# Deferring the second layer norm to the outputs of the first two feed-forward units

## The reference, cut to what matters

```python
h = memory_cross_attention(x, mem, xa_wq, xa_wkv, xa_wo)       # ends with "@ wo"
x = layer_norm(ALPHA * x + h, ln2_g, ln2_b)                    # the second norm
u = causal_dwconv(x @ w_up, conv_w, conv_b)                    # 3 taps, 5632 columns
g, val = split(u); h = (gelu(g) * val) @ w_down
x = layer_norm(ALPHA * x + h, ln3_g, ln3_b)                    # the third norm
```

## Time and profile before

| | us |
|---|---|
| median of 3 runs | 903.06 |
| lowest, highest | 900.4, 904.37 |
| the profiled execution | 901.49 |
| its span, first to last instruction | 899.7 |

### The profile page before, as it was taken

One profiled execution on the slowest core, in us unless ns is written; L12 is line 12 of the kernel. 1 busy time (PEld: TensorE's weight loads), 2 busy tenths in 40 slices (PEclk: granted clock), 3 DMA queues, 4 the chain that ended last, 5 costly groups with the idle time before them and its releaser, 6 DMA issues.

```text
span 899.7 us, 15840 instructions
## 1 busy us (share of the span) xinstructions
PE 857.0 (95%) x6396; PEld 807.8 (90%) x6396; DVE 651.3 (72%) x1011; ACT 503.2 (56%) x723; POOL 7.6 (1%) x17
## 2 busy tenths in 40 slices
PE   8989998999899999999997989999899899999997
PEld 7869987889799999999996989898899899999886
DVE  5765697678668888887867896687797866665453
ACT  5644447355447666655446657777657654444442
POOL 0200000000000000000000000000000000000000
PEclk9989999989998999999988999999999799999999
DMA  9973567747062766567752576475575276775751
GB/s 337 241 226 104 160 229 221 212 154 238 24 184 74 231 186 185 174 208 255 260 188 70 154 222 200 129 224 166 160 225 175 66 250 219 233 233 186 162 212 47
DMA packets 139592, 166.89 MB, mean 186 GB/s; under 512 B 5520, under 2 KB 123280, under 8 KB 139520
## 3 DMA queue, kind: packets, MB, share of 16 engines
q1 hardware_dynamic: 137712, 162.82, 57.8%
q0 software_dynamic: 720, 2.02, 1.2%
q10 hardware_dynamic: 1088, 1.05, 0.3%
HBM read 164.62 MB, written 1.25 MB: 184 GB/s over the span
## 4 chain that ended last, share of the span: by engine, by line
PE 63%; DVE 14%; ACT 7%; issue 3%; DVEq 0%; ACTq 0%
PE ps L519 62%; DVE lor L1608 5%; DVE FA L1608 3%; ACT hir L1103 2%; DVE FA L1611 1%; DVE FA L1614 1%; DVE X L1608 1%; DVE INL L1608 1%; DVE raw L1625 0%; ACT FA L1294 0%; ACT L1447 0%; ACT FA L1227 0%; ACT FA L1489 0%; DVE X L1611 0%; ACT L1118 0%
## 5 line engine op out<-in xcount | busy, mean ns | idle before, releaser
L1608 DVE TENSOR_TENSOR lor<-raw,hir 128x1024 fp32r<-128x1024 f32 (+1 forms) x267 | 309.8, 1177 | 115.2 <-ACT hir L1103 110.2
L1103 ACT ACTIVATE hir<-raw 128x1024 fp32r<-128x1024 f32 (+1 forms) x257 | 260.3, 1032 | 124.9 <-PE ps L519 104.4
L519 PE MATMUL ps<-INH,hir 128*128 128x256 f32 (+1 forms) x1064 | 306.7, 288 | 4.2 <-ACT INH L1269 2.5
L519 PE MATMUL ps<-INH,lor 128*128 128x256 f32 (+1 forms) x1064 | 302.5, 284 | 3.4 <-DVE lor L1608 3.4
L519 PE MATMUL ps<-INL,hir 128*128 128x256 f32 (+1 forms) x1064 | 303.2, 285 | 1.2 <-DVE INL L1608 0.9
L519 PEld LDWEIGHTS ps<-INH,hir 128*128 128x128 f32 x1064 | 204.7, 192 | 7.4 <-issue 5.8
L519 PEld LDWEIGHTS ps<-INH,lor 128*128 128x128 f32 x1064 | 204.4, 192 | 5.4 <-DVE lor L1608 4.4
L519 PEld LDWEIGHTS ps<-INL,hir 128*128 128x128 f32 x1064 | 204.0, 192 | 2.5 <-DVE INL L1608 2.4
L519 PE MATMUL ps<-HIH,lor 128*128 128x256 f32 x688 | 195.9, 285 | 4.3 <-DVE lor L1608 4.3
L519 PE MATMUL ps<-HIH,hir 128*128 128x256 f32 x688 | 198.2, 288 | 0.0
L519 PE MATMUL ps<-HIL,hir 128*128 128x256 f32 x688 | 194.6, 283 | 0.0
(11 more groups left out here) (270 smaller groups left out, 792.8 us busy)
## 6 DMA issues: line engine op xcount, KB each, us to landing
raw<-in_w_in SPq DMA_DIRECT2D x64, 512.0 KB, 4.7
raw<-in_mod_wT SPq DMA_DIRECT2D x48, 512.0 KB, 4.5
raw<-in_ffn_w_up SPq DMA_DIRECT2D x44, 512.0 KB, 4.6
raw<-in_w_ffn_in SPq DMA_DIRECT2D x44, 512.0 KB, 4.7
raw<-in_w_ffn_out SPq DMA_DIRECT2D x22, 512.0 KB, 4.6
raw<-in_ffn_w_down SPq DMA_DIRECT2D x20, 512.0 KB, 4.8
raw<-in_xa_wkv SPq DMA_DIRECT2D x16, 512.0 KB, 4.2
raw<-in_xa_wq SPq DMA_DIRECT2D x8, 512.0 KB, 4.9
```

What stands on the lines that cost most here:

```text
L519: return e.matmul(o, l, r, start=start, stop=stop, skip_group_check=True)
L1103: e.activation(hi, src, ACT.Copy).then_inc(*w_hi.up(i))
L1608: return e.tensor_tensor(o, a, b, op)
```

## The change

`up 0` and `up 11` no longer multiply the normed x2. DVE and ACT make, right after each residual, high and low part of X times the norm's weight (`gained`, two slices per `xo` unit), and two extra columns hold the weight vector and the bias vector themselves (`gains`). PE multiplies these 258 columns. The extra outputs are the products of the weights with the two vectors, and `settle` then computes for each unit (output minus mean by first extra column) by the reciprocal deviation plus second extra column, into a buffer UP, from which the convolutions of step 0 read. The other twenty units still read the normed x2, which is made as before, now in four groups of two slices, and behind the steps that the diff shows. The sums and spreads stand on PE between slices of the pair. The pair uses two accumulator banks per unit.

At the head of the program:

```diff
+LATE = (("up", 0), ("up", 11)), (("q", 2), ("k", 2))
...
+        xg1, xg2 = (Inp(n, HIHX[:, 0:8, :], HILX[:, 0:8, :]) for n in ("xg1", "xg2"))
```

In PE's program:

```diff
+            def late_norm(name, keys, x):
+                g = late_g(keys, x, 2)
+                steps_of(g, 1)
+                row_sums(name, 3, X[:, 6:8, :])
+                steps_of(g, 1)
+                spread_bank((name, "mu"), SN[:, 0:2])
+                steps_of(g, 1)
+                spread_bank((name, "r"), SN[:, 6:8])
+                run(g)
...
-            layer_norm("n2")
-            run(units_g([("up", 0), ("up", 11)], 8, x2))
+            late_norm("n2", LATE[0], xg2)
...
-                    unit(("up", 11 + c), 8, x2)
+                    unit(("up", 11 + c), 8, x2, pool=att if c == 1 else lin)
```

In ACT's program (inside the loop over k stand the two high parts of x2 and the two affine writes of X, as before; the loop is followed by `ahead.more()`):

```diff
+            def gained(x, name, gn, c, free):
+                for k in (2 * c, 2 * c + 1):
+                    w.wait_ge(dve.at((name, "x", c)), vec_in.at(0), mm.at(free))
+                    e.activation(x.hi[:, k, 0:T], X[:, k, :], ACT.Copy, scale=V(gn, k)).then_inc(...)
+            def late_norm(name, gn, bn, inp, free, keys):
+                late = ahead.units_g(keys, 8)
+                next(late)
+                w.wait_ge(dve.at((name, "var")))
+                e.activation(SN[:, 4:6], SN[:, 2:4], ACT.Sqrt).then_inc(...)
+                w.wait_ge(mm.at((name, "mu")), mm.at((name, "early")))
+                e.activation(MB, bank[name, "mu"][:, 0:T], ACT.Copy).then_inc(...)
+                for k in (0, 2, 4, 6):
+                    if k == 4:
+                        run(late)
...
+                ahead.more()
+            def settle(i, key, dst):
+                for j in range(2):
+                    w.wait_ge(dve.at((key, "normed")))
+                    e.activation(dst[:, j, :], dst[:, j, :], ACT.Identity, scale=-1.0, bias=GB2[i][j][:, 1:2]).then_inc(...)
...
+                square("n2", c, X[:, 2 * c:2 * c + 2, :], ...)
+                gained(xg2, "n2", "ln2_g", c, "xg2 free")
...
-            layer_norm("n2", "ln2_g", "ln2_b", x2, "x2 free")
+            late_norm("n2", "ln2_g", "ln2_b", x2, "x2 free", LATE[0])
+            for i, key in enumerate(LATE[0]):
+                settle(i, key, UP[:, 2 * i:2 * i + 2, :])
+                if i == 0:
+                    ahead.more()
...
-            ahead.units([("up", 0), ("up", 11)], 8)
```

In DVE's program (mean, variance and reciprocal are as before):

```diff
+            def gained(x, gn, c):
+                for k in (2 * c, 2 * c + 1):
+                    w.wait_ge(act.at((x.name, "hi", k)))
+                    stt(x.lo[:, k, 0:T], X[:, k, :], V(gn, k), x.hi[:, k, 0:T].bitcast(F32), MUL, SUB).then_inc(...)
+            def late_norm(name, x, inp, free, keys):
+                late = ahead.units_g(keys, 8)
...
+                next(late)
+                for k in (0, 2, 4, 6):
+                    d = X[:, k:k + 2, :]
+                    w.wait_ge(act.at((name, "mean row")), act.at((x.name, "hi", k + 1)), dve.at((x.name, "lo", k + 1)))
+                    tt(d, d, over(MB, 2), SUB).then_inc(*dve.up())
+                    w.wait_ge(mm.at((name, "r")), dve.last())
+                    tt(d, d, over(br[:, 0:T], 2), MUL).then_inc(...)
+                    if k:
+                        low(k - 2)
+                    if k == 2:
+                        run(late)
+                low(6)
+                ahead.more()
+            def settle(name, i, key, dst, *free):
+                for j in range(2):
+                    b, vs = bank["unit", key, j], GB2[i][j]
+                    w.wait_ge(mm.at(("unit", key, j)))
+                    e.tensor_copy(vs, b[:, T:T + 2]).then_inc(*dve.up())
+                    stt(dst[:, j, :], MB, vs[:, 0:1], b[:, 0:T], MUL, SUB).then_inc(...)
+                tt(dst, dst, over(br[:, 0:T], 2), MUL).then_inc(...)
...
+            for i, key in enumerate(LATE[0]):
+                settle("n2", i, key, UP[:, 2 * i:2 * i + 2, :], ...)
+                if i == 0:
+                    ahead.more()
```

More of the change, by code:

```diff
@@ L435, in build @@
         SN = SMALL[:, 424:436]
+        GB2 = [[SMALL[:, 436 + 4 * i + 2 * j:438 + 4 * i + 2 * j] for j in range(2)] for i in range(2)]
         SS, VP, VR4, SD4, RR = (CH[:, a:a + n] for a, n in ((0, 4), (4, 2), (6, 2), (8, 2), (10, 2)))
@@ L487, in last_matmul @@
                 return "read", i
-            return ("unit", key, 1) if kind == "wide" or key in (("q", 2), ("k", 2)) else ("unit", key)
+            return ("unit", key, 1) if kind == "wide" or any(key in keys for keys in LATE) else ("unit", key)
         before_in_slot, seen = {}, {}
@@ L536, in halves, with units_g @@
                 return act.at((x.name, "hi", k)), dve.at((x.name, "lo", k))
-            def units_g(keys, kt, x, outs=columns):
-                bs = [lin.get(("unit", key), bank) for key in keys]
+            def units_g(keys, kt, x, outs=columns, pool=lin):
+                bs = [pool.get(("unit", key), bank) for key in keys]
                 oo = [outs(b) for b, _ in bs]
@@ L567, in units_g, with unit @@
                         yield
-            def unit(key, kt, x, outs=columns):
-                run(units_g([key], kt, x, outs))
+            def unit(key, kt, x, outs=columns, pool=lin):
+                run(units_g([key], kt, x, outs, pool))
             def wide_g(key, kt, x, pool=lin, apart=0):
@@ L804, in layer_norm, with late_free @@
                 spread_bank((name, "r"), SN[:, 6:8])
+            def late_norm(name, keys, x):
[7 more added lines that the diff above has]
+                run(g)
+                for key in keys:
+                    lin.release(("unit", key, 0))
+            def late_free(keys):
+                for key in keys:
+                    att.release(("unit", key, 1))
             for c in range(4):
                 unit(("wout", c), 8, mix)
+            mm.mark("xg2 free")
             mm.mark("x1 free")
@@ new lines, in late_norm, with low @@
+            def late_norm(name, x, inp, free, keys):
+                late = ahead.units_g(keys, 8)
+                w.wait_ge(mm.at((name, "sums")))
+                e.tensor_copy(SN[:, 0:4], bank[name, "sums"][:, 0:4]).then_inc(*dve.up(("out", (name, "sums")), ((name, "mu"), "factor")))
+                then("mean")
+                tt(SN[:, 8:10], SN[:, 0:2], SN[:, 0:2], MUL).then_inc(*dve.up())
+                then("mean squared")
+                stt(SN[:, 2:4], SN[:, 2:4], LN_EPS, SN[:, 8:10], ADD, SUB).then_inc(*dve.up())
+                then("variance")
+                ts(SN[:, 2:4], SN[:, 2:4], LN_EPS, None, MAX).then_inc(*dve.up((name, "var")))
+                w.wait_ge(act.at((name, "deviation")))
+                e.reciprocal(SN[:, 6:8], SN[:, 4:6]).then_inc(*dve.up(((name, "r"), "factor")))
+                next(late)
+                br = bank[name, "r"]
+                def low(k):
+                    w.wait_ge(act.at((name, "affine", k)), mm.at(free))
+                    tt(inp.lo[:, k:k + 2, :], X[:, k:k + 2, :], inp.hi[:, k:k + 2, :].bitcast(F32), SUB).then_inc(*dve.up(*inp.los(k, 2)))
+                for k in (0, 2, 4, 6):
+                    d = X[:, k:k + 2, :]
+                    w.wait_ge(act.at((name, "mean row")), act.at((x.name, "hi", k + 1)), dve.at((x.name, "lo", k + 1)))
+                    tt(d, d, over(MB, 2), SUB).then_inc(*dve.up())
+                    w.wait_ge(mm.at((name, "r")), dve.last())
+                    tt(d, d, over(br[:, 0:T], 2), MUL).then_inc(*dve.up((name, "normed", k), ("out", (name, "r"))))
+                    if k:
[4 more added lines that the diff above has]
+                ahead.more()
@@ new lines, in settle @@
+            def settle(name, i, key, dst, *free):
+                br = bank[name, "r"]
+                for j in range(2):
+                    b, vs = bank["unit", key, j], GB2[i][j]
+                    w.wait_ge(mm.at(("unit", key, j)))
+                    e.tensor_copy(vs, b[:, T:T + 2]).then_inc(*dve.up())
+                    w.wait_ge(dve.last(), act.at((name, "mean row")), *free)
+                    stt(dst[:, j, :], MB, vs[:, 0:1], b[:, 0:T], MUL, SUB).then_inc(
+                        *dve.up(("out", ("unit", key, j))))
+                w.wait_ge(dve.last(), mm.at((name, "r")))
+                tt(dst, dst, over(br[:, 0:T], 2), MUL).then_inc(*dve.up((key, "normed"), ("out", (name, "r"))))
@@ L1957, in vector, with up_values @@
                 stats("n2", c, ("n1", "early"))
-            layer_norm("n2", "ln2_g", "ln2_b", x2, "x2 free")
+                gained(xg2, "ln2_g", c)
             dve.mark("before up")
+            late_norm("n2", xg2, x2, "x2 free", LATE[0])
+            for i, key in enumerate(LATE[0]):
+                settle("n2", i, key, UP[:, 2 * i:2 * i + 2, :], mm.at("before up"), dve.at("before up"), act.at("before up"))
+                if i == 0:
+                    ahead.more()
+            def up_values(key):
+                if key in LATE[0]:
+                    i = LATE[0].index(key)
```

(4 more changed lines are left out.)

58 lines of the change are left out of this document (46 added, 12 removed).

## The result

The changed kernel takes 913.06 us in the median of 4 executions (910.91 to 915.62), beside 903.71 us for the kernel before (4 executions, 900.4 to 905.59). The ratio is 1.0116 with an interval of 1.0084 to 1.0148. The change makes this kernel slower by about 10 us (the medians differ by 9.4, the ratio says 1.16%). The profiled execution took 911.32 us, its span is 909.5.

What follows compares the result with a forecast made beforehand. It took PE as busiest, but DVE, with 1.4 us spare behind the norm, as decisive: `up 2` done at 312.1 instead of 302.35, 9.7 us later, so 901.49 becomes 911.2; range 904 to 916.

Steps and rivals of the forecast that it cites:

- the walk: Predicted chain through DVE and ACT from the residuals to `up 2`, done at 312.1 instead of 302.35; chance 0.76.
- Scaled sum: At the `xo` units: 0.80 us more on ACT and DVE, last residual at 265.8 and not 265.04; cost 0.8 us.
- Sums: PE's norm sums behind 12 matmuls: done at 268.65, small chain to the reciprocal 1.25 us, so 269.9.
- Spreads behind 24 matmuls: PE in the norm: 24 matmuls at 4.48 us, then spreads of 0.6 and 0.93; DVE's first product at 274.6.
- the nearest row: Third norm's profile row: the same 24 matmuls behind one-column sums took 4.48 us, clock 0.69, taken for the spreads.
- x2: Norming in two halves: ACT's eight instructions end at 279.4, eight more at 288.2; low part of `up 12` at 290.5.
- Settling: `up 0` and `up 11` on DVE 1.97 us each, ACT 0.9, alternating with `up 12`'s splits; ACT done at 298.3.
- Step 0: Taps, table load and GELU to 302.9; then `up 2`'s high part done at 303.9, low part at 305.1.
- `up 2`: Second low part at 309.1, last 24 matmuls 2.83 us, done at 312.1; cold clock after the gap costs nothing.
- over 5: Sign: PE waits over 5 us before `up 2`, ended by ACT's split; shorter than 3 us would refute the prediction.
- The first rival: Works as meant: PE's gap in the norm filled, all behind moves up, 896.7 us; chance 0.08.
- The second rival: Gain given back at once, no more: waits in `up 1` and `up 12`, `up 2` split in time; 902, chance 0.10.

Runs made afterwards that it cites:

- x5: Kernel before plus the scaled-sum work of ACT and DVE, results unread; 901.71 us, ratio 1.0009.
- x4: Changed kernel without settling of `up 0` and `up 11` on both engines, so their convolutions read raw sums; 900.53 us, ratio 1.0001.
- x1: Changed kernel with DVE settling both units before the last low part of x2 and the splits of `up 12`; 903.26 us, ratio 1.002.
- x6: Changed kernel's instructions reordered: spreads directly behind sums, all slices normed before low parts, settling early on DVE, splits earlier; 897.77 us, ratio 0.9958.
- x3: Changed kernel with the second chunk of `up 12` and first of `up 2` split ahead of settling on ACT and DVE; 907.43 us, ratio 1.0071.

## Why the prediction was right

It had 911.2 us with the walk's mechanism most likely; the profiled execution took 911.32, the median is 913.06, and the `up 2` it put at 312.1 is done at 312.51. The path and its waits are those of the walk. That the time came out within 0.2 us is partly luck, as several terms were off by 0.5 to 1.0 us in both directions. By its steps:

1. *Scaled sum.* Last residual at 265.80, as said; x5 shows the 0.80 us by itself.
2. *Sums.* The last ones start at 267.45 and the reciprocal is ready near 269.9. Right.
3. *Spreads behind 24 matmuls.* The clock fell, as at the third norm. The windows of the changed kernel:

```profile
268.00:270.00 2.00, 2.00 (x12) 0.54 0.75 223
270.00:272.00 2.00, 2.00 (x13) 0.61 0.07 17
272.00:274.00 2.00, 2.00 (x20) 1.00 0.83 257
```

   The 1.2 GHz level was over by 272, sooner than in the nearest row: the 24 matmuls and the first spread took from 268.52 to 273.29, 4.8 us for 5.1, and the second spread gave its product after 0.65 instead of 0.93. The first product starts at 273.94, not 274.6; the term was 0.6 us too large. The rule of the Trainium skill, page "TensorE: Matmul & The Clock Gate", section "Part 1: The HAM clock gate", that the gate follows how busy PE has been, had the product 1.65 us before 274.6 as the prediction read it, at about 272.9. The measured start lies between the two. The clock speaks against that reading, as the records have PE busy 2.00 of 2.00 us at 0.54; so the busy time of the records alone does not keep the clock up here.
4. and 5. *x2.* ACT is idle for 2.89 us between the halves, and its high part of `up 12` starts at 288.04, which the walk had at 288.2. By here the 0.7 us by which the first product came early are almost used up: eight of ACT's instructions took 4.34 us each time (274.66 to 279.00, 283.80 to 288.13), and the walk had 4.1.
6. *Settling.* DVE's two settlings took 290.36 to 292.33 and 295.50 to 297.47, 1.97 us each, in a row with ACT's splits as walked. This is the step that carries the result: x4 puts 9.4 us on it and x1 shows that 7.6 of these are the order alone.
7. *Step 0.* GELU at 301.69 and the high part done at 303.27; predicted 302.9 for the end of the GELU and 303.9. The 0.6 us are an error of this step: the walk had the table load wait for DVE's taps (301.0), but ACT begins it at 300.40, beside them.
8. *`up 2`.* Here two errors cancel in part. The low part of the second chunk was ready at about 308.5 (307.31 and half of 2.36), not 309.1. But the prediction costed the cold clock after the gap at nothing, since it would lie ahead of that low part. It doesn't, quite:

```profile
304.00:306.00 2.00, 1.32 (x6) 0.50 0.11 23
306.00:308.00 2.00, 2.00 (x11) 0.50 0.73 240
308.00:310.00 2.00, 2.00 (x15) 0.72 0.13 26
```

```profile
309.47 0.28 PE L523 MATMUL ps<-INH,hir 128*128 128x256 f32 x1
```

   PE was through its first 24 matmuls only at 309.47, 1.0 us after the low part was ready. So the end of `up 2` is set by the cold clock and not by DVE. That this term was "nothing" is the largest wrong term, worth 1.0 us. The wait before `up 2` itself was 4.79 us, where "over 5" was named as a sign and under 3 as the refutation.

PE's side was right as well: the pair ends at 281.1 (predicted 281.5), 3.8 us sooner than the 284.9 read for before, and all of it is lost again in waits. The first rival, 896.7, failed at the point that the prediction named: the low part of `up 2` had to be ready at 291.4 and came at 304.6 (303.40 and 1.23). The rule of the Trainium skill, page "Perfetto Trace Analysis", section "Identifying the Most-Contended Engine", to optimize the engine with the highest occupancy first, did not carry over to this order of work: filling PE's gap costs 10 us in the changed kernel. In x6, where DVE and ACT keep up, the same fill goes with a gain of 3.8. The second rival, `up 2` split in time, was tried as x3 for the first of its two chunks. With that split early the next one is late, and 1.7 us come back in the stage and not the 8 to 9 that the rival needs (911.2 less 903.4 or 901.7). So the position of the split behind the GELU was not all that was wrong. Both chunks of `up 2` in time with the settling left in place were not run.

The term that the prediction did not have is how much of the chain is order. It walked the path and found it 13.7 us late for the low part of `up 2`; it did not ask which of these microseconds are work. x6 does the same work as the changed kernel and is 12.4 us sooner at the mark.

## What to carry over

Before work is moved off the engine with the fewest gaps, walk the programs of the engines that are to take it, in order, up to the next thing that the busy engine needs. Two engines that alternate on short steps can set the end while each of them is idle for a third to a half of the time, as DVE and ACT here; windows in which no engine is full are a sign of it. A step whose result is needed late (here the settling, for step 0) is better put where its engine waits anyway than between the halves of an exchange (high part, low part) that feeds the busy engine: in x1 this gave back 7.6 of 10.2 us.

## What the runs showed of the hardware that was not expected

PE's granted clock fell behind the one-column sums although the records show no gap of PE. In the changed kernel the sums run from 265.71 to 268.5; the clock is 1.00 up to 268 and 0.54 in the window from 268 to 270, with PE busy 2.00 of 2.00 us. In x6, with a pause of 0.26 us and eight spreads of 128 columns behind the same sums, it stayed at the low level until 275 (0.60, 0.50, 0.50 and 0.69 in the four windows from 268 to 276), three microseconds longer than in the changed kernel, and x6 is the fastest all the same.

In x5 the clock is at 0.50 in every window from 268 to 280, and in the kernel before only from 270 to 276. That profiled execution lost 3.3 us in this stage where only 0.8 were added, and it is one execution. The mean granted clock differs between executions of one and the same kernel, and the time goes with it: of 19 executions of the kernel before on one chip, the three under 899 us (897.59, 898.41, 898.94) have a mean granted clock of 0.974, and the longest, 904.54, has 0.965. A single profiled execution can so be some microseconds off without any edit, and whether the delay in x5 brought the clock down is not shown.
